# Bank takes, the branch behind the experts and the order of three splits in a hand-scheduled two-block kernel

## The reference

```
h = h + g1 * y                                            # y: the layer's mixer
h = h + g2 * ffn(rms_norm(h, norm2_g[l]) * (1 + sc2) + sh2)

# layer 1: ffn = mixture, all 8 experts weighted by gates (zero off the two best)
out = gates[:, 0:1] * swiglu(xt, w1[0], w3[0], w2[0])
for e in range(1, N_EXPERTS):
    out = out + gates[:, e:e + 1] * swiglu(xt, w1[e], w3[e], w2[e])

# second block
xn = rms_norm_2(h, norm_mix_pre)
proj = xn @ w_in                    # qkv of the dilated attention | q_c | kv_c, k_pe | gates
gates = jax.nn.sigmoid(proj[..., IN_A + IN_B:] + b_gate)
o_a = mixer_dilated(qkv_a, pos) @ w_o_a
o_b = mixer_mla(q_c, kv_c, k_pe, pos, mla_q_norm, mla_w_uq, mla_kv_norm, mla_w_ukv) @ w_o_b
mix = (g_a * o_a + g_b * o_b) @ w_out
h = h + rms_norm_2(mix, norm_mix_post)
ff = jnp.square(jax.nn.relu(rms_norm_2(h, norm_mlp_pre) @ w_ff1)) @ w_ff2
h = h + rms_norm_2(ff, norm_mlp_post)
```

## Time and profile before

| | |
|---|---|
| median of 3 runs | 1808.86 us (1803.52, 1808.86, 1812.89) |
| profiled execution, its own time | 1805.37 us |
| its span | 1803.4 us |
| mean granted clock of TensorE | 0.967 |
| TensorE / VectorE / ScalarE / GpSimd busy | 92% / 69% / 46% / 8% |
| read from HBM | 331 MB, 184 GB/s over the span |

### The profile page before, as it was taken

How to read it: one execution, slowest core, us unless ns; L and a number is a source line. 1 busy time by engine, 2 the same in 40 slices (tenths; PEclk the granted TensorE clock), 3 DMA queues, 4 the chain that set the end, 5 groups by cost and what they waited for, 6 DMA issues and landing times. The chain is left out here.

```text
span 1803.4 us, 21412 instructions
## 1 busy us (share of the span) xinstructions
PE 1662.9 (92%) x8686; PEld 1414.6 (78%) x8686; DVE 1240.3 (69%) x1618; ACT 832.8 (46%) x1015; POOL 141.5 (8%) x142
## 2 busy tenths in 40 slices
PE   5989879899999999789889999999979989889998
PEld 2868767788788887787678888787869967779986
DVE  6477764577755555776688888899886576666643
ACT  6344332422212224343367766767745444545532
POOL 2110001100110011420100000000020000000000
PEclk9998989999999999899979999999998999999999
DMA  8342322355655442212249899898956522235553
GB/s 338 95 164 94 140 101 86 117 193 204 245 210 189 174 152 76 71 48 71 95 182 356 323 332 343 306 353 297 356 198 214 199 88 87 80 144 187 185 189 117
DMA packets 59064, 333.60 MB, mean 185 GB/s; under 512 B 14530, under 2 KB 14849, under 8 KB 25680
## 3 DMA queue, kind: packets, MB, share of 16 engines
q1 hardware_dynamic: 54640, 311.06, 47.5%
q0 software_dynamic: 2592, 14.57, 2.5%
q10 hardware_dynamic: 1728, 6.54, 1.0%
HBM read 331.00 MB, written 1.13 MB: 184 GB/s over the span
## 5 line engine op out<-in xcount | busy, mean ns | idle before, releaser
L2085 DVE TENSOR_TENSOR wlo__61<-raw__60,whi__62 128x2048 fp32r<-128x2048 f32 (+2 forms) x64 | 145.3, 2270 | 71.5 <-ACT whi__62 L1530 71.3
L2085 DVE TENSOR_TENSOR wlo__65<-raw__64,whi__66 128x2048 fp32r<-128x2048 f32 (+3 forms) x64 | 141.1, 2205 | 73.0 <-ACT whi__66 L1530 72.8
L1530 ACT ACTIVATE whi__62<-raw__60 128x2048 fp32r<-128x2048 f32 (+2 forms) x64 | 118.9, 1858 | 86.2 <-DMA raw__60<-in_ffn_w 43.2
L1530 ACT ACTIVATE whi__66<-raw__64 128x2048 fp32r<-128x2048 f32 (+3 forms) x64 | 115.4, 1803 | 82.1 <-DMA raw__64<-in_ffn_w 32.2
L2085 DVE TENSOR_TENSOR wlo__69<-raw__68,whi__70 128x2048 fp32r<-128x2048 f32 (+4 forms) x50 | 109.2, 2184 | 23.9 <-ACT whi__70 L1530 23.7
L2118 DVE SCALAR_TENSOR_TENSOR wsum__71<-raw__68,silu_rows 128x1024 f32<-128x1024 f32 x84 | 99.9, 1220 | 22.4 <-DMA raw__68<-in_ada_w 21.8
L3228 POOL TENSOR_TENSOR keep__58<-keep__58,keep__59 128x1 f32<-128x1 f32 (+3 forms) x48 | 53.6, 1119 | 592.7 <-DVE keep__58 L2159 592.7
L1530 ACT ACTIVATE whi__70<-raw__68 128x2048 fp32r<-128x2048 f32 (+4 forms) x50 | 90.5, 1809 | 19.7 <-DMA raw__68<-in_w_ff 11.4
L2085 DVE TENSOR_TENSOR wlo__235<-raw__234,whi__236 128x2048 fp32r<-128x2048 f32 (+1 forms) x24 | 50.7, 2111 | 11.8 <-ACT whi__236 L1530 11.8
L918 PE MATMUL ps<-ffn__129,wlo__61 128*128 128x512 f32 (+1 forms) x128 | 47.6, 372 | 6.4 <-ACT ffn__136 L1573 4.1
L2374 DVE TENSOR_REDUCE keep__58<-ps 128x1 f32<-128x256 f32 (+1 forms) x88 | 44.4, 516 | 12.8 <-PE ps L1168 7.6
(11 more groups left out here) (1171 smaller groups left out, 5298.2 us busy)
## 6 DMA issues: line engine op xcount, KB each, us to landing
raw__68<-in_moe_w SPq DMA_DIRECT2D x24, 1024.0 KB, 5.2
raw__60<-in_moe_w SPq DMA_DIRECT2D x24, 1024.0 KB, 5.8
raw__68<-in_ada_w SPq DMA_DIRECT2D x16, 1024.0 KB, 5.0
raw__64<-in_moe_w SPq DMA_DIRECT2D x16, 1024.0 KB, 5.4
raw__230<-in_moe_w SPq DMA_DIRECT2D x16, 1024.0 KB, 6.2
raw__234<-in_moe_w SPq DMA_DIRECT2D x16, 1024.0 KB, 7.0
raw__144<-in_ada_w SPq DMA_DIRECT2D x13, 1024.0 KB, 6.7
raw__68<-in_ada_w POOLq DMA_DIRECT2D x10, 1024.0 KB, 5.2
```

The lines of the kernel that those rows point to most:

```text
L1530: e.activation(t.hi(), t.raw(), ACT.Copy).then_inc(*did("hi", i))
L2085: e.tensor_tensor(t.lo(), t.raw(), t.hi().bitcast(F32), ALU.subtract).then_inc(*did("lo", i))
```

## The change

1. `proj` takes the bank of each t at that t's first product, not all of them ahead of the first.
2. ScalarE's `norm_by_token` raises `ahead` to 2 at t = 3 only for N "o", no more for "f".
3. The last expert's output of r = 0 is moved behind the branch. `again` gets a function `finish`, which is written into both arms; in the second copy the bookkeeping (`book.repeat`) isn't counted again. TensorE's flag is loaded at the end of expert 1. For the last expert (and all of r = 1) VectorE multiplies y by the gate rows in its banks (`yg`) before it is split, and the last sum goes straight into h: the sum of the experts before was already added to h's copy by GpSimd (`hpre`). The two adds of `moe_h` and the tile `TR` are gone; who waited for `moe_h` waits for the last sums.
4. Behind the norm's turning, the ring `"8"` is set to bank 6 ahead of the second block's projections.
5. In the latent attention `ahead` is 0 up to unit lag + 2 and 2 from then on, on ScalarE and VectorE.

The diff, cut to its core:

```diff
@@ -162,11 +162,12 @@
         self.at, self.now, self.sems, self.counting, self.by = {}, Counter(), {}, True, {}
+        self.repeat = False
...
         self.now[sem] += by
-        if self.counting:
+        if self.counting and not self.repeat:
             assert (name, *key) not in self.at, (name, key)
@@ -639,18 +637,29 @@
-    def again(e, at, taken, body):
+    def again(e, at, taken, body, finish=lambda: None):
         outer, before = at["due"], Counter(book.now)
         with e.If(taken == 1):
-            at.update(due=outer.inner(), gate="again")
+            at["due"] = outer.inner()
+            finish()
+            at["gate"] = "again"
             body(1)
-            at.update(due=outer, gate="")
+        after = Counter(book.now)
+        book.now, book.repeat = Counter(before), True
         with e.Else():
-            for name, n in list(book.now.items()):
-                if n > before[name]:
-                    if before[name]:
-                        e.wait_ge(book.sems.get(name), before[name])
-                    e.sem_inc(book.sems.get(name), n - before[name])
+            at.update(due=outer.inner(), gate="")
+            finish()
+            for name, n in after.items():
+                now = book.now[name]
+                if n > now:
+                    if now:
+                        e.wait_ge(book.sems.get(name), now)
+                    e.sem_inc(book.sems.get(name), n - now)
+        at["due"], book.now, book.repeat = outer, after, False
+    def summed_up():
+        return [("acc", 1, 7, t, half) for t in range(2) for half in range(2)]
@@ -662,7 +671,7 @@
         if stage == "moe":
-            return [("moe_h", t)]
+            return [("acc", 0, 7, t, half) for half in range(2)]
         return [("res", stage, half, t) for half in range(2)]
@@ -855,7 +864,7 @@
         def done(name, *key):
-            if book.counting:
+            if book.counting and not book.repeat:
                 n = place[name, *key] = state["tile"]
@@ -924,12 +933,14 @@
         def proj(key, x, nt, K, src, n, ready, ring="8", stop=True, between=None):
-            bs = [take(ring, *key, t) for t in range(nt)]
+            bs = []
             kc = 2048 // n
...
                 for t in range(nt):
+                    if k0 == 0:
+                        bs.append(take(ring, *key, t))
                     for k in range(k0, k0 + m):
@@ -1420,17 +1431,39 @@
                         turn_hidden(r, ex, 2)
-            scatter(r, 7)
+                if not r and ex == 1:
+                    state["taken"] = ask(e, state)
+            if r:
+                scatter(r, 7)
...
         state["loads"] = (2, *slot_m)
-        again(e, state, ask(e, state), experts)
+        rings, held = dict(turn_of), dict(holder)
+        def last_scattered():
+            if not book.repeat:
+                return scatter(0, 7)
+            past = dict(turn_of), dict(holder)
+            for d, x in ((turn_of, rings), (holder, held)):
+                d.clear()
+                d.update(x)
+            scatter(0, 7)
+            for d, x in zip((turn_of, holder), past):
+                d.clear()
+                d.update(x)
+        def once_more(r):
+            experts(r)
+            for s, n in state["due"](*summed_up()):
+                e.wait_ge(s, n)
+        again(e, state, state["taken"], once_more, last_scattered)
         state["loads"] = None
...
         norm_turn("s", 0)
+        turn_of["8"] += -turn_of["8"] % 8 + 6
         w_in = W["w_in_2"]
@@ -1593,6 +1626,8 @@
             for i in A.steps():
+                if st == "a3":
+                    at["ahead"] = 2 if i > A.lag + 2 else 0
                 if st == "a0":
@@ -1736,7 +1771,7 @@
             for t in range(4):
-                if t == 3:
+                if t == 3 and N == "o":
                     at["ahead"] = 2
@@ -1907,27 +1942,33 @@
                 feed(("y", r, ex, 10))
-                for half in range(2):
-                    high("yph", (r, ex, half), YP[0][:, half * 512:half * 512 + 512], bank("y", r, ex, half),
-                         ("y", r, ex, 10), *xg_free(r, ex, "scat", 1, 1))
-            feed(("scat", r, 7, 1, 1))
+                if r or ex < 7:
+                    output_hi(r, ex)
+        def output_hi(r, ex):
+            for half in range(2):
+                high("yph", (r, ex, half), YP[0][:, half * 512:half * 512 + 512], bank("y", r, ex, half),
+                     *([("yg", r, ex, half)] if r or ex == 7 else [("y", r, ex, 10)]), *xg_free(r, ex, "scat", 1, 1))
         experts(0)
-        again(e, at, at["taken"], experts)
+        def once_more(r):
+            experts(r)
+            for s, n in due(*summed_up()):
+                e.wait_ge(s, n)
+        again(e, at, at["taken"], once_more, lambda: output_hi(0, 7))
         feed(("scat", 1, 7, 1, 1))
...
         norm_turned("s", 0)
-        free = [("moe_h", t) for t in range(2)] + [("scat", 1, 7, 1, 1)]
+        free = summed_up() + [("scat", 1, 7, 1, 1)]
         for s, n in due(*free):
...
             *did("bg", by=16))
-        for s, n in due(("moe_h", 0), ("moe_h", 1)):
-            e.wait_ge(s, n)
         e.dma_start(MSK2, cst_d[:, DILM:DILM + 1536]).then_inc(*did("msk2", by=16))
@@ -2902,21 +2945,12 @@
                     past = [("acc", r, ex - 1, t, half)] if ex else [("acc", 0, 7, t, half)] if r else []
-                    past = past + ([("hpre", t), *spr(11)] if (r, ex) == (0, 7) else [])
-                    if r and (ex, t, half) > (0, 0, 0):
-                        n = ex * 4 + t * 2 + half - 1
-                        past.append(("acc", 1, n // 4, n // 2 % 2, n % 2))
+                    past = past + ([("hpre", t)] if (r, ex) == (0, 7) else [])
+                    if r or ex == 7:
+                        dst = h_t[t][:, half * 512:half * 512 + 512]
                     for s, n in due(("scat", r, ex, t, half), ("sel",), ("mcnt",), *past):
                         e.wait_ge(s, n)
-                    gates = GBC[:, D + half * 512:D + half * 512 + 512]
-                    if r:
-                        e.scalar_tensor_tensor(out=TR, in0=b, scalar=g, in1=gates, op0=ALU.mult, op1=ALU.mult).then_inc(*link())
-                        for s, n in linked():
-                            e.wait_ge(s, n)
-                        m = e.tensor_tensor(dst, dst, TR, ALU.add)
-                    elif ex == 7:
-                        m = e.scalar_tensor_tensor(out=dst, in0=b, scalar=g, in1=gates, op0=ALU.mult, op1=ALU.mult)
-                    elif ex == 0:
+                    if (r, ex) == (0, 0):
                         m = e.tensor_scalar(dst, b, g, None, ALU.mult)
@@ -2944,19 +2978,28 @@
                 feed(("y", r, ex, 10))
-                for half in range(2):
-                    hs = slice(half * 512, half * 512 + 512)
-                    low("ypl", (r, ex, half), YP[1][:, hs], bank("y", r, ex, half), YP[0][:, hs], ("yph", r, ex, half))
-                    empties(("y", r, ex, half), ("ypl", r, ex, half))
-            scattered(r, 7)
+                if r or ex < 7:
+                    output_lo(r, ex)
+            if r:
+                scattered(r, 7)
+        def output_lo(r, ex):
+            for half in range(2) if r or ex == 7 else ():
+                for s, n in due(("y", r, ex, 10), *spr(11)):
+                    e.wait_ge(s, n)
+                yb = bank("y", r, ex, half)
+                e.tensor_tensor(yb, yb, GBC[:, D + half * 512:D + half * 512 + 512], ALU.mult).then_inc(*did("yg", r, ex, half))
+            for half in range(2):
+                hs = slice(half * 512, half * 512 + 512)
+                low("ypl", (r, ex, half), YP[1][:, hs], bank("y", r, ex, half), YP[0][:, hs], ("yph", r, ex, half))
+                empties(("y", r, ex, half), ("ypl", r, ex, half))
+        def last_output():
+            output_lo(0, 7)
+            scattered(0, 7)
         experts(0)
-        again(e, at, at["taken"], experts)
-        for t in range(2):
-            for s, n in due(("acc", 1, 7, t, 0), ("acc", 1, 7, t, 1), ("hpre", t)):
-                e.wait_ge(s, n)
-            e.tensor_tensor(h_t[t], h_t[t], MACC[t], ALU.add).then_inc(*did("moe_h", t))
+        again(e, at, at["taken"], experts, last_output)
         at["ahead"] = 1
@@ -3321,7 +3364,7 @@
             norm_rsqrt("s", t)
-        for s, n in due(("scat", 1, 7, 1, 1), ("moe_h", 0), ("moe_h", 1)):
+        for s, n in due(("scat", 1, 7, 1, 1), *summed_up()):
             e.wait_ge(s, n)
```

4 lines of the change are left out of this document (1 added, 3 removed).

## The result

The changed kernel takes 1818.20 us (median of 7 runs, 1816.50 to 1820.16) against 1811.22 us of the kernel before (7 runs beside it): a ratio of 1.0046, with a 95% interval of 1.0033 to 1.0059. By this ratio that is +8.3 us (+6.0 to +10.7); the two medians stand 7.0 us apart. The forecast was 1817 us and +8.1 us. The profiled execution took 1817.01 us, its span is 1815.2 us.

A forecast was written before the change was run, and what follows sets the result against it. TensorE, busy for 92% of 1803.4 us, was taken to bound the kernel. The terms -2.9 - 1.8 + 0 + 0 - 3.5 + 11.3 + 6.0 - 1.0 gave +8.1 us, forecast 1817 us, range 1803 to 1828.

The forecast's parts named there:

- The two bank waits: Ring shift: TensorE stands 9.9 us ahead of the gates and 4.3 ahead of `uq`; with low clock +11.3 and +6.0 us.
- The rival without these waits: Ring shift: neither bank wait comes, so the kernel is 9.2 us faster, 1799.7 us; chance 0.10.
- The first projection: First projection (q), at 45.63: TensorE's wait for bank 3 goes, -2.9 us (-1.3 to -3.1).
- The second half of the feed-forward output: First feed-forward output, second half: TensorE's 1.71 us wait for a bank goes, -1.8 us (-1.9 to -1.3).
- The projection at 718: 256-column projection at 717.97: 2.76 us of wait go but end in a longer later wait, 0 (0 to +2).
- half of it carries: Rival: gains of banks at first product and of the last attention carry half of 5.7 us, 1820 us; chance 0.08.
- Part 2: Feed-forward norm: starts 2.6 us earlier, but the second weight tile is ready only at about 335.7; 0 (-1 to +1).
- Part 3: End of the experts: scatter starts 3.0 us behind the last product, next projection earlier; -3.5 us (-5.5 to -1).
- the way that the prediction put beside its own: End of the experts: by the skill's 108 ns branch the scatter starts at 1346.1, worth 0.8 us more.
- if the clock stays up: End of the experts: next projection is 5.3 us ahead with the clock up, about 2.5 if it falls.
- Part 5: Last attention: TensorE starts 2.4 us earlier, but the splits at unit 6 can take it back; -1.0 us (-2.4 to +1).
- The scale: Whole kernel: the median of three runs, 1808.86, stands 3.5 us above the profiled execution, turning 1813.5 into 1817 us.

The follow-up runs named there:

- uq_back: Changed kernel with ring "8" moved on by two banks only ahead of `uq`, which has banks 0 and 1 again: 1812.08 us, ratio 1.0009.
- proj_only: Kernel before with only the projection's banks each taken at its first product: 1808.68 us, ratio 0.9990.
- f_back: Changed kernel with the tile split ahead of the feed-forward norm's last piece put back: one profiled execution, 1815.61 us.
- no_a3: Changed kernel with the last attention's two tiles again split ahead of its first units: 1819.15 us, ratio 1.0054.
- best1: Changed kernel with ring "8" moved on by two banks ahead of the latents, and the last attention's splits ahead of its first units again: 1802.96 us, ratio 0.9949.
- end_only: Kernel before with only the new end of the experts (last expert's output behind the branch): 1807.53 us, ratio 0.9980.
- ring_only: Kernel before with only ring "8" set to bank 6 behind the norm's turning: 1826.04 us, ratio 1.0093.

## Why the prediction was right, point by point

- **The time and the sign** came out as forecast: 1818.2 for 1817, +8.3 for +8.1. The two bank waits were right; that the sum agrees so closely is luck. Between the profiled executions the steps are 1.0 us worse than forecast at part 2, 0.7 worse between the turned head and the last y, 4.1 worse in the last attention (mostly the lucky execution of before) and 1.9 better at part 3. The parts run alone make -1.8 (part 1) -3.6 (part 3) +16.8 (part 4) -1.8 (part 5), by their ratios, and with +1.0 for part 2 from the trace +10.6, at the upper edge of the changed kernel's interval (+6.0 to +10.7); of these, parts 1 and 5 aren't clear of zero.
- **The two bank waits** carry it. Their place and length were as written: 9.55 us for 9.9, and 4.28 for 4.3. The releaser was as written for the first; for the second the profile names another, and uq_back had to decide. The low clock behind the first cost 1.4 us and not 2.2 (0.61 from 1433.6 to 1437.5, then 1.00 up to 1441); the wait ahead of the turned latents got shorter by 0.5 us, not 0.8. Timed: 11.5 for 11.3 and 6.1 for 6.0 by the medians, 10.5 and 6.7 by the ratios. The rival without these waits (chance 0.10) fell with the first profile.
- **The first projection.** -2.7 us in the changed kernel's trace and in proj_only's, for -2.9. TensorE started at 43.66 and not 42.9, since this execution had been 0.7 us late before; the clock stayed up (1.00 from 43.6 to 47.0), as supposed, and the second stop for pieces (0.68 us) came.
- **The second half of the feed-forward output.** -2.0 us for -1.8, right. **The projection at 718**: gained 3.0 us, given back at once to VectorE's chain, right. The low clock behind that wait came too (1.9 us in proj_only, 1.6 in the changed kernel), which the sum had at 0 and its bound at +2. Part 1 measured -1.8 alone for the -4.7 of the sum: this term was mis-sized, and by the time the rival "half of it carries" (chance 0.08) was nearer for part 1.
- **Part 2**, 0 (-1 to +1): +1.0 by the table and by f_back, at the edge of its range. The second weight tile came when the prediction had it: its product starts at 333.61 in an execution that is 2.1 us ahead of before's at this norm, and 335.7 was predicted. What wasn't priced is the low clock behind the wait of 2.43 us.
- **Part 3: the sum was right and a step was wrong.** "Its instruction takes 3.52 us in the one row there is, so I take 3.0 us behind the last product" failed. The row's length is right; what was overlooked is that TensorE's sequencer reaches the branch before the queued matmuls are done, so none of it lies behind the last product. The scatter started 2.24 us behind it (2.2 by the way that the prediction put beside its own). The section of the Trainium skill named there would have given the better start of the scatter here, by a figure that the trace contradicts. The early start didn't show in the sum, as the changed kernel's scatter ran at the low clock (0.63 us a matmul for 0.39 before): from the last product to the next projection 10.45 us passed, for 10.3 in the prediction. Behind that the clock stayed up, and -5.4 us came where the prediction had written 5.3 "if the clock stays up" and -3.5 as the mean. In the kernel with this part alone the clock fell from 1357 on, the start waited for bank 0, and it is -3.2 by the trace and -3.6 by the time (-0.7 to -6.3).
- **Part 5**, -1.0 (-2.4 to +1): -1.0, -2.4 and -2.1 by the medians, none clear of zero. The mechanism was half of it. The 2.35 us of wait go, and a wait of 3.06 us behind the two splits comes at unit 6, as feared; the rest is the clock, which the prediction held for a side matter.
- **The scale.** The profiled execution of before lies 3.5 us below the median of the three runs then known. Its last attention had the high clock for most of its time. Carrying the difference of 3.5 us over to the changed kernel was wrong: its own profiled execution lies only 1.2 us below its median. It took 1817.0 us where the prediction's way gives 1813.5. The two misses cancel in the median: luck.

## What to carry to other kernels

A ring's start position is a promise to every later user of the same banks: before it is moved, list who holds each bank at each take and when its last reader is done, for the small rings that share banks as well. A gain of 1 to 2.5 us at one place doesn't tell of the 17 us that the same line costs from 80 us later on, and moving the ring back by two banks behind the place that wanted the shift took the loss away. A long sequencer instruction costs nothing while matmuls are still queued ahead of it, or while the engine waits for another engine anyway: look at what released the next matmul, not at the instruction's length.

## What the runs showed of the hardware that was not expected

- TensorE's branch instruction took 3.37 to 3.80 us in the fourteen profiled kernels, while those of SyncE, ScalarE and VectorE took 55, 50 and 72 ns. It overlapped matmuls that were already queued, for 3.5 us in the changed kernel. Why it is so much longer than the others stays open.
- The same attention, instruction for instruction, took 21.7 to 28.5 us in fourteen profiled runs, and the length went with the granted clock (0.85 to 0.58 over the stretch in the nine shown). Kernels whose two splits stand ahead of its first units mostly spread more from run to run (the kernel before over 11 to 13 us, no_a3 over 11, best1 over 15, end_only over 10, but proj_only over 6 and ring_only over 4) than those with part 5 (2.5 to 7). What decides the clock there in a single run stays open.
